# Shifts of three LayerNorms on GpSimd, an output projection in another order, and a last LayerNorm through TensorE, in a two-layer HGRN2/GLA trunk

## The reference, cut to what matters

```python
for l in range(DEPTH):                                   # DEPTH = 2, D_MODEL = 2048
    sh1, sc1, g1, sh2, sc2, g2 = jnp.split(mod, 6, axis=-1)   # from silu(c) @ w_ada
    h = x * (1.0 + sc1) + sh1
    y, s = hgrn2_mixer(h, ...) if l % 2 == 0 else gla_mixer(h, ...)
    x = layer_norm(ALPHA * x + (1.0 + g1) * y, ln_w[l, 0], ln_b[l, 0])
    h = x * (1.0 + sc2) + sh2
    y = jnp.square(jax.nn.relu(h @ w_up[l])) @ w_down[l]
    x = layer_norm(ALPHA * x + (1.0 + g2) * y, ln_w[l, 1], ln_b[l, 1])
# layer_norm: xc = x - mean(x); xc * rsqrt(mean(xc * xc) + EPS) * w + b
```

## Time and profile before

| what | value |
|---|---|
| median of 3 runs | 3139.27 us |
| profiled execution, its own time | 3138.88 us |
| its span | 3137.1 us |
| granted TensorE clock, mean | 0.989 |
| TensorE (PE) busy | 3062.4 us, 98% |
| VectorE (DVE) busy | 1753.8 us, 56% |
| ScalarE (ACT) busy | 1305.1 us, 42% |
| GpSimd (POOL) busy | 313.4 us, 10% |

### The profile page before, as it was taken

The page is one execution under the profiler, slowest core; times in us unless marked ns, Lnnn a source line. Parts: engine busy times, 40 slices in busy tenths (PEclk is TensorE's granted clock), DMA queues, the critical chain, the costliest instruction groups (busy, mean ns, idle before and its releaser), DMA issues.

```text
span 3137.1 us, 66335 instructions
## 1 busy us (share of the span) xinstructions
PE 3062.4 (98%) x26988; PEld 2856.9 (91%) x26988; DVE 1753.8 (56%) x2471; ACT 1305.1 (42%) x1702; POOL 313.4 (10%) x290
## 2 busy tenths in 40 slices
PE   7899999999999999999999899999999999999998
PEld 3689999889899999999999889987999999999998
DVE  2477777765744444444445666666574444454446
ACT  1355555553443333333333544444353343343433
POOL 0022222221300000000001401100130000000000
PEclk8899999999999999999999999999999999999999
DMA  9998777888777676776775765675445555555542
GB/s 374 319 301 260 250 255 253 265 286 288 253 258 232 210 254 212 229 245 201 241 247 180 251 227 159 208 232 189 156 138 165 168 165 165 168 163 167 167 164 78
DMA packets 541644, 685.68 MB, mean 219 GB/s; under 512 B 22226, under 2 KB 469258, under 8 KB 541066
## 3 DMA queue, kind: packets, MB, share of 16 engines
q1 hardware_dynamic: 484402, 625.43, 61.1%
q10 hardware_dynamic: 56960, 56.21, 5.4%
HBM read 650.88 MB, written 30.67 MB: 217 GB/s over the span
## 4 chain that ended last, share of the span: by engine, by line
PE 92%; DVE 3%; DMA 3%; ACT 1%; issue 0%; POOL 0%; SPq 0%; DVEq 0%; ACTq 0%; POOLq 0%
PE main L549 27%; PE main L551 26%; PE main L550 26%; PE bank L561 5%; DMA raw<-in_w_ada 2%; PE bank L691 1%; PE bank L1144 1%; DVE z L2346 0%; DVE z L2350 0%; PE bank L1129 0%; PE bank L579 0%; DVE w_lo L1852 0%; PE bank L1115 0%; DVE a_lo L2380 0%; DMA raw<-in_hg_w_in 0%
## 5 line engine op out<-in xcount | busy, mean ns | idle before, releaser
L1852 DVE TENSOR_TENSOR w_lo<-raw,w_hi 128x1024 fp32r<-128x1024 f32 x804 | 993.5, 1238 | 1192.4 <-ACT w_hi L1266 1189.5
L1266 ACT ACTIVATE w_hi<-raw 128x1024 fp32r<-128x1024 f32 x804 | 850.4, 1059 | 1537.0 <-PE main L551 1419.2
L549 PE MATMUL main<-a_hi,w_hi 128*128 128x288 f32 x4240 | 1287.5, 304 | 17.1 <-DVE a_lo L2380 13.8
L551 PE MATMUL main<-a_hi,w_lo 128*128 128x288 f32 x4240 | 1255.2, 296 | 0.0
L550 PE MATMUL main<-a_lo,w_hi 128*128 128x288 f32 x4240 | 1254.4, 296 | 0.0
L549 PEld LDWEIGHTS main<-a_hi,w_hi 128*128 128x128 f32 x4240 | 801.1, 189 | 60.1 <-issue 34.9
L550 PEld LDWEIGHTS main<-a_lo,w_hi 128*128 128x128 f32 x4240 | 800.9, 189 | 4.6 <-issue 1.9
L551 PEld LDWEIGHTS main<-a_hi,w_lo 128*128 128x128 f32 x4240 | 800.8, 189 | 0.0
L549 PE MATMUL main<-act_hi,w_hi 128*128 128x288 f32 x2048 | 606.7, 296 | 0.0
L551 PE MATMUL main<-act_hi,w_lo 128*128 128x288 f32 x2048 | 605.4, 296 | 0.0
L550 PE MATMUL main<-act_lo,w_hi 128*128 128x288 f32 x2048 | 602.2, 294 | 0.0
(11 more groups left out here) (319 smaller groups left out, 2059.7 us busy)
## 6 DMA issues: line engine op xcount, KB each, us to landing
raw<-in_w_ada SPq DMA_DIRECT2D x384, 512.0 KB, 6.8
raw<-in_w_up SPq DMA_DIRECT2D x256, 512.0 KB, 3.8
raw<-in_w_down SPq DMA_DIRECT2D x256, 512.0 KB, 3.4
raw<-in_hg_w_in SPq DMA_DIRECT2D x128, 512.0 KB, 6.6
raw<-in_gla_w_in SPq DMA_DIRECT2D x100, 512.0 KB, 3.9
raw<-in_hg_w_out SPq DMA_DIRECT2D x32, 512.0 KB, 7.7
gl_s<-in_state_gla ACTq DMA_DIRECT2D x32, 512.0 KB, 5.5
out_new_gla_sample<-gl_s ACTq DMA_DIRECT2D x32, 512.0 KB, 4.7
```

The costliest lines, as they stand in the source:

```text
L549: mm(out, hi, x_hi[:, kb, :], start=kb == 0, stop=False)
L551: last = mm(out, lo, x_hi[:, kb, :], start=False, stop=kb == KB - 1)
L1266: F(w_hi[:, st.split_slot(g)].rearrange("p k n -> p (k n)"), raw[:, slot, :], ACT.Copy).then_inc(hi_ready, 1)
L1852: V.tensor_tensor(w_lo[:, s].rearrange("p k n -> p (k n)"), raw[:, slot, :], w_hi[:, s].rearrange("p k n -> p (k n)").bitcast(F32), ALU.su ...
```

## The change

Three parts.

1. In layer_norm for the LayerNorms 0, 1 and 2 the shifts of the last two chunks (blocks 8 to 15) are made by GpSimd in a new function shift, called at the head of affine, behind ln_spread. VectorE waits for ln_shifted before the pieces 3 and 4.
2. In GLO, ScalarE and VectorE do their share of the GLA tail ahead of the cast and split of the same step. In VectorE's gl_step the mask goes ahead of the state update, and in GLO silu_mul goes behind both.
3. Behind LayerNorm 3 z is neither shifted nor scaled. TensorE multiplies the provisionally centered z by a diagonal matrix of ln_w (y_turn; this transposes too) and adds a product of 33 rows that holds the mean and the bias (y_terms). rstd is brought to the partitions as a column and is the scale of the eviction, which ScalarE and VectorE share. SP stores the groups. Of 9 groups the last holds all the sample tokens, in 4 column groups of TensorE. The diagonal is made by VectorE in the last MLP iteration; two rows of weights are loaded by SP behind a memset of GpSimd.

```diff
@@ tensor: layer_norm, and the tail
+        def layer_norm(i, filler=None, last_one=False):
             for c in range(4):
+                if last_one and c == 3:
+                    y_turn(0)
...
-            else:
+            elif not last_one:
                 for _ in range(16):
                     mm(b6[:, 0:P], ones[:, :], ones[:, :], start=True, stop=True)
...
+        def y_turn(g):
...
+            if g < 8:
+                c, i = divmod(g, 2)
+                for j in range(4):
+                    mm(bank[:, j * P:(j + 1) * P], z[:, 4 * c + j, i * P:(i + 1) * P], diag[:, 4 * c + j, :], start=j == 0,
+                       stop=False, skip_group_check=True)
+            else:
+                for kb in range(KB):
+                    c, j = divmod(kb, 4)
+                    mm(bank[32 * c:32 * c + 32, j * P:(j + 1) * P], z[:, kb, TP:T], diag[:, kb, :], start=j == 0, stop=False,
+                       skip_group_check=True, tile_position=(0, 32 * c))
+        def y_terms(g):
...
+                last = mm(bank[:, :], terms[0:33, i * P:(i + 1) * P], wb[0:33, c * 512:(c + 1) * 512], start=False, stop=True,
+                          skip_group_check=True)
...
+        layer_norm(3, last_one=True)
+        y_turn(1)
+        y_turn(2)
+        pe.wait_ge(y_log, 1)
...
+        y_turn(3)
+        for g in range(9):
+            y_terms(g)
+            if g + 4 < 9:
+                y_turn(g + 4)
@@ scalar and vector: out_projection (vector's shown)
             for s in range(32):
+                for x in ((2 * s, 2 * s + 1) if s < 5 else (10, 11, 12, 13) if s == 5 else ()):
+                    tail(x)
                 split(st, 0, s + AHEAD)
                 if s == 1:
                     low_part(e, 2, o_buf[:, 8:12, :])
-                for x in ((2 * s, 2 * s + 1) if s < 5 else (10, 11, 12, 13) if s == 5 else ()):
-                    tail(x)
@@ vector: layer_norm
-            shift(8, 12)
             split(splits, 0, 3)
             low(2)
+            dve.wait_ge(ln_shifted, 2 * i + 1)
             piece(3)
+            dve.wait_ge(ln_shifted, 2 * i + 2)
             if splits is LOW:
-                shift(12, 16)
                 low(3)
...
             split(splits, 0, 4)
-            shift(12, 16)
             low(3)
@@ vector: gl_step
-            if s == 0:
+            if s == 0 and own:
                 silu_mul(...)
+            if s <= 5:
+                gl_mask(pn, s + 2)
             if s <= 6:
                 gl_state(pn, s + 1)
-            if s <= 5:
-                gl_mask(pn, s + 2)
+            if s == 0 and not own:
+                silu_mul(...)
@@ gpsimd
+        def shift(i):
+            pool.wait_ge(ln_spread, i + 1)
+            for c in (2, 3):
+                k = slice(4 * c, 4 * c + 4)
+                nc.gpsimd.tensor_tensor(z[:, k, :], z[:, k, :], mu[:, :].unsqueeze(1).to_broadcast([P, 4, T]), ALU.subtract
+                                        ).then_inc(ln_shifted, 1)
         def affine(i):
+            shift(i)
```

## The result

The changed kernel takes 3155.36 us as the median of 5 runs (3152.55 to 3158.39), the kernel before 3139.57 us on the same chip (5 runs, 3139.05 to 3142.74): a ratio of 1.005, with a 95% interval of 1.004 to 1.0061, or +15.8 us. The forecast was 3148.5 us, +9 us. The direction and the place were right, the size was not. The profiled execution took 3156.65 us, with a span of 3154.6 us.

What follows compares the result with a forecast made beforehand. TensorE, busy 98% of the span, was taken as the bound, so only its waits and the serial tail count. 10.3 + 1.5 - 4.4 + 2.0 = +9.4 us gave a forecast of 3148.5 us, own range 3144 to 3156 us.

Steps and rivals of the forecast that it cites:

- Part 1: Behind three LayerNorms: GpSimd's two shifts delay VectorE 1.84 us each, TensorE 3.7 us; +10.3 us in all.
- g: Length of GpSimd's new 128x1152 shift instruction behind the LayerNorms: taken as 2.3 us, ends 2.1 and 3.2 us.
- the 0.14 us of the rule: On VectorE: a held-up instruction finishes as if begun when GpSimd was done, less 0.14 us; part of g - 0.46 us.
- The gain of 0.8 us for the removed shifts: On VectorE: about 0.5 us behind the second LayerNorm, 0.3 us behind the third, 0 behind the first.
- The clock: On TensorE behind the three LayerNorms: more half-speed stretches from longer waiting, +1.5 us, ends 0 and 4.
- Part 2: Output projection of layer 1: first wait goes, second falls to about 0.8 us; -4.4 us, ends -6 and -3.
- the third rival: VectorE keeps its place, tail at its low end, projection at -6, its half-speed stretch gone: -9 us, 3130 us; chance 0.05.
- Part 3: Tail behind the last matmul: TensorE sets it, last issue later; +2.0 us, ends -0.6 and +3.5.
- the bare sum: Tail's last issue at 3136.1 us against 3134.76 us, +1.4 us, before any cost for changing between shapes.
- The first: Behind the LayerNorms: VectorE keeps its place or GpSimd gives way; sum -3.2 us, 3136 us; chance 0.15.
- The second: Behind the LayerNorms: only one of two GpSimd shifts gets ahead of the first chunk; +2.8 us, 3142 us; chance 0.12.
- The fourth: GpSimd's instruction takes 3.2 us and the tail is at its upper end: +19 us, 3158 us; chance 0.05.

Runs made afterwards that it cites:

- e5: The kernel before with only GpSimd's shifts behind LayerNorms 0, 1 and 2, started once the second piece's low part is ready: 3150.11 us, ratio 1.0031.
- part 2 alone: The kernel before with only the new order in the output projection of layer 1: 3135.94 us, ratio 0.9989.
- part 1 alone: The kernel before with only the two shifts moved to GpSimd behind LayerNorms 0, 1 and 2: 3155.19 us, ratio 1.0049.
- e7: The kernel before with only the last LayerNorm through TensorE, its products of terms widened from 33 to 128 rows with zeros: 3141.09 us, ratio 1.0003.

## Why the prediction was right in direction and short by 7 us

**Part 1, mechanism right, size off.** The step said that GpSimd gets in at VectorE's first two pauses, and that VectorE is late by g - 0.46 us each time. Both happened, at the instructions named. The term that was mis-sized is g. VectorE's scaling ended at 822.45 + 3.08 = 825.53 us; less its own 0.76 us, and with the 0.14 us of the rule, GpSimd was done at 824.91 us. It can have begun 0.29 us ahead of the end of VectorE's shift (822.42 us), so its own length is 2.78 us; the second, which ended at 827.99 us, gives 2.75 us. GpSimd's own record of the first shift, 3.68 us from 821.23 us on, ends at 824.91 us too, which confirms the 0.14 us; by the earlier trace rows it would have been 0.16 us (780.98 - 1.24 = 779.74 us against 779.90 us), a slip that changes nothing. I took 2.3, near the slope of the earlier trace rows, and nothing in those rows showed that it holds from 288 to 1152 columns. That 2.78 us gives back the measured 2.32 us is no test, since it was worked out from it; the test is that the second shift gives the same length, and that e5's, by its own record, took 2.69 us. The estimate from the Trainium skill's page (GPSIMD Engine Reference, Engine selection) was 2.7 us, nearer than mine; the ends of my range, 2.1 and 3.2 us, held it. Six times 0.48 us are 2.9 us of the miss.

The start of TensorE is late by 4.8 us, 0.2 us more than the two delays. From the start of the second chunk's scaling to the product 2.48 us pass (828.26 to 830.74) where it was 2.28 us (823.70 to 825.98): with GpSimd's affine steps beside them L1940 took 0.49 us for 0.23 and the low part 0.98 for 0.77, while L1941 took 0.22 us, where it had met such a step before and taken 0.49. That is some 0.6 us for the three places.

The gain of 0.8 us for the removed shifts didn't come. From the first product L549 to the 120th behind it there pass 68.2 us before and 68.4 us after behind LayerNorm 1, and 50.3 us both times behind LayerNorm 2. VectorE now waits there for ScalarE:

```profile
2315.02 1.40 DVE L2454 TENSOR_TENSOR a_lo<-ln_h,a_hi 128x1152 fp32r<-128x1152 f32 x1 [1.37 <-ACT a_hi L1369]
```

I had seen that releaser behind LayerNorm 1 alone and counted 0.5 us there; it holds behind both, and the value is 0.

**The clock.** I added 1.5 us. In the changed kernel TensorE is granted half speed for 6.8 us from 828.1 us on, for 13.7 us from 1736.0 us on and for 6.8 us from 2306.0 us on, longer than before behind all three. Much of it lies where TensorE waits, so it costs little there: the products behind LayerNorm 0 end up 0.3 us later than their first one, those behind LayerNorm 1 0.1 us. One stretch of 3.4 us at 1725.8 us covers the products of LayerNorm 1's mean and variance, ahead of ln_spread, which took 1.0 us more than before; it stands in the profiled executions of all four kernels with part 1, and besides only in that of part 2 alone. In all it is 1.4 us, so this term holds. Part 1 then makes 10.3 + 1.5 + 2.9 + 0.6 + 0.8 - 0.1 = 16.0 us; part 1 alone measured +15.9 us.

**Part 2, right in sign, for the wrong reason in part.** -4.4 us were forecast, -3.4 us measured alone. The step that failed is the layout of the new order with old durations: it had no term for the stores. In the kernel before, the store of state 1 landed at 2168.78 us, just ahead of the state update at 2169.25 us that needed its buffer. That wait was hidden by the split and the low part ahead of the update, and it came out when they were moved away: L1169 waits 3.41 us, where I had laid out 0.8 us. In the changed kernel, 0.7 us were won in the stretch itself, and 1.6 us because the half-speed stretch of the earlier trace rows fell away; I had left that one to the third rival (Part 2 of the prediction calls it the second). Inside the stretch the profiled execution of the kernel before had no half speed at all, but the six other kernels with the old order and the old loads had 3.4 to 10.2 us of it, and the three with part 2 and the old loads 0 to 3.4 us. So a good part of part 2's gain is likely fewer half-speed stretches, which the prediction had priced at nothing. How much of its -3.4 us alone is order and how much is clock, the runs don't separate.

**Part 3, size off.** +2.0 us were forecast with an upper end of +3.5, +3.4 us measured. Three terms moved. The change between shapes costs 0.2 us each time, not 0.1, and comes ten times, not 16: five pairs at 2.15 - 1.76 = 0.39 us make 1.9 us, as e7 shows by taking it away. y_turn(0) delays the statistics by 1.0 us, not 0.6. And the sample group's 32 passes took 2.4 us (3144.11 to 3146.50) and not 2.9: they run one behind the other, as taken. With the 1.4 us of the bare sum that is 1.4 + 1.9 + 0.4 - 0.5 = 3.2 us; the table of differences has 1.0 + 2.6 = 3.6 us.

**The rivals.** The first, that VectorE keeps its place, fell: it would have shown the scaling at 0.76 us. The third rests on it and fell too. The second, one shift only, fell with L1940 at 2.52 us. The fourth had the right two causes, a longer GpSimd instruction and the upper end of the tail, with a chance of 0.05. The length g goes into the sum six times, so its ends of 2.1 and 3.2 us alone were worth 6.6 us; the value between them deserved more doubt than any other. The measured time lies at the upper end of the forecast's own range, 3144 to 3156 us.

## What to carry to other kernels

Before work is moved to GpSimd, ask two things: does it read SBUF, and who waits for VectorE in that stretch. The subtractions here, which read, were paid for by VectorE at its next pause in all but about 0.46 us, so a shift of 1.35 us moved away from VectorE came back as 2.3 us on the path; the memsets, which only write, were free. And when a wait is taken away, look at when the buffer behind it came free: here a store's landing stood 0.5 us ahead of the instruction that needed it, and took over much of the gain. Of the versions run, part 2 alone is the fastest, 0.1% below the kernel before.

## What the runs showed of the hardware

- A GpSimd instruction of two operands over 128x1152 needs 2.7 to 2.8 us where VectorE needs 1.35 us, and VectorE's instructions with two SBUF operands stand still for it (0.76 us became 3.08 us); two memsets of 128x2304 beside the same instructions cost them nothing.
- The 16 DMA engines carried 401 to 404 GB/s in stretches of 5 us, stores and loads mixed, in three orders of issue. A store of 512 KB landed 7.1 us behind its issue with a load and another store issued shortly ahead of it, and 3.6 us behind it without that load.
- A product of 33 rows between products of 128 rows costs about 0.2 us at each change; 128 rows with zeros don't.
- TensorE's half-speed stretches (1.2 GHz) fall differently from kernel to kernel in the same code: 0 to 10.2 us of 23.6 to 27.3 us in the output projection's old order.
